# Forgetting attention from DRAM rows: split keys and queries, rounded value products, eight score groups a head

## The reference, cut to what matters

```python
k = rms_norm(k.reshape(N, T, N_HEADS, HEAD_DIM), k_norm)
q = rms_norm((xn @ w_q[j]).reshape(N, T, N_HEADS, HEAD_DIM), q_norm[j])
s = jnp.einsum('nqhd,nkhd->nhqk', q, k, preferred_element_type=jnp.float32) * (HEAD_DIM ** -0.5)
s = s + (c_q - c_k)            # c: running sums of the log forget values, by head
s = jnp.where(causal, s, NEG_INF)
p = jax.nn.softmax(s, axis=-1)
return jnp.einsum('nhqk,nkhd->nqhd', p.astype(v.dtype), v)
```

## Time and profile before

| | us |
|---|---|
| runs: lowest, median, highest | 2987.47, 2991.85, 2993.87 |
| profiled execution, its own time | 2989.96 |
| its span, first to last instruction | 2987.8 |
| PE busy | 2810.3 |
| DVE busy | 1178.7 |
| ACT busy | 779.7 |
| POOL busy | 154.1 |

### The profile page before, as it was taken

One profiled execution on the slowest core, in us unless ns is written; L12 is line 12 of the kernel. 1 busy time (PEld: TensorE's weight loads), 2 busy tenths in 40 slices (PEclk: granted clock), 3 DMA queues, 4 the chain that ended last, 5 costly groups with the idle time before them and its releaser, 6 DMA issues.

```text
span 2987.8 us, 41222 instructions
## 1 busy us (share of the span) xinstructions
PE 2810.3 (94%) x16738; PEld 2701.7 (90%) x16738; DVE 1178.7 (39%) x1258; ACT 779.7 (26%) x1163; POOL 154.1 (5%) x97
## 2 busy tenths in 40 slices
PE   6999999999999999999878888857999999999999
PEld 5999999999999999889876777745899999999998
DVE  4444434233142233433356666534344233242331
ACT  4111121111011122462454444434321011111111
POOL 3000020000000002110111000000010000000000
PEclk8999999999999999999998898979999999999999
DMA  3111111111111111123200111033011111111112
GB/s 96 48 46 42 43 51 42 43 43 49 42 42 49 43 43 47 39 72 86 54 28 20 53 26 27 23 107 110 22 43 49 43 43 49 42 42 44 47 42 73
DMA packets 251776, 145.79 MB, mean 49 GB/s; under 512 B 29424, under 2 KB 243248, under 8 KB 251682
## 3 DMA queue, kind: packets, MB, share of 16 engines
q1 hardware_dynamic: 232578, 135.47, 15.6%
q10 hardware_dynamic: 19104, 8.99, 1.1%
HBM read 130.91 MB, written 13.45 MB: 48 GB/s over the span
## 4 chain that ended last, share of the span: by engine, by line
PE 81%; DVE 6%; issue 4%; DMA 3%; ACT 3%; POOL 2%; ACTq 1%; SPq 0%; DVEq 0%; POOLq 0%
PE ps L377 71%; PE ps L655 3%; DMA inv_sums<-inv_rows 2%; DVE max_parts L593 2%; PE ps L820 1%; PE ps L743 1%; PE ps L631 1%; PE ps L632 1%; POOL t L412 1%; DMA inv_rows<-inv_spread 1%; DVE q_all L683 1%; DVE q_lo_hi L517 1%; DVE k_hi_lo L521 1%; DVE row_max L593 1%; POOL squares L1346 1%
## 5 line engine op out<-in xcount | busy, mean ns | idle before, releaser
L362 DVE TENSOR_TENSOR w_lo<-w_raw,w_hi 128x1024 fp32r<-128x1024 f32 x192 | 246.7, 1285 | 1259.5 <-ACT w_hi L354 1259.5
L377 PE MATMUL ps<-x_hi,w_hi 128*128 128x358 f32 x2688 | 593.9, 329 | 16.8 <-DVE x_lo L405 16.7
L377 PE MATMUL ps<-x_hi,w_lo 128*128 128x358 f32 x2688 | 590.9, 328 | 0.0
L377 PE MATMUL ps<-x_lo,w_hi 128*128 128x358 f32 x2688 | 589.4, 327 | 0.0
L354 ACT ACTIVATE w_hi<-w_raw 128x1024 fp32r<-128x1024 f32 x192 | 203.6, 1060 | 1322.8 <-PE ps L377 1320.4
L377 PEld LDWEIGHTS ps<-x_hi,w_hi 128*128 128x128 f32 x2688 | 465.2, 190 | 20.3 <-DVE x_lo L405 10.4
L377 PEld LDWEIGHTS ps<-x_lo,w_hi 128*128 128x128 f32 x2688 | 466.6, 190 | 0.0
L377 PEld LDWEIGHTS ps<-x_hi,w_lo 128*128 128x128 f32 x2688 | 466.4, 190 | 0.0
L377 PE MATMUL ps<-hid_hi,w_hi 128*128 128x358 f32 x1920 | 423.4, 329 | 3.2 <-DVE hid_lo L1150 3.2
L377 PE MATMUL ps<-hid_hi,w_lo 128*128 128x358 f32 x1920 | 420.8, 327 | 0.0
L377 PE MATMUL ps<-hid_lo,w_hi 128*128 128x358 f32 x1920 | 420.0, 327 | 0.0
(11 more groups left out here) (215 smaller groups left out, 2166.2 us busy)
## 6 DMA issues: line engine op xcount, KB each, us to landing
w_raw<-in_mlp_w SPq DMA_DIRECT2D x128, 512.0 KB, 4.0
w_raw<-in_conv_w_in SPq DMA_DIRECT2D x24, 512.0 KB, 3.8
w_raw<-in_w_kv SPq DMA_DIRECT2D x16, 512.0 KB, 3.8
k_page<-in_cache_k SPq DMA_DIRECT2D x16, 512.0 KB, 3.8
v_page<-in_cache_v SPq DMA_DIRECT2D x16, 512.0 KB, 4.0
inv_sums<-inv_rows SPq DMA_DIRECT2D x16, 260.0 KB, 3.4
w_raw<-in_conv_w_out SPq DMA_DIRECT2D x8, 512.0 KB, 3.9
out_k_prompt<-out_tiles ACTq DMA_DIRECT2D x8, 512.0 KB, 3.9
```

The source lines that it names most:

```text
L362: dve.tensor_tensor(WL[:, s], RAW[:, s], WH[:, s].bitcast(F32), ALU.subtract).then_inc(w_lo, 1)
L377: mm = pe.matmul(PS[:, G * s + g, 0:GW], w[:, s, k], x[:, k, g * GW:(g + 1) * GW], start=(k == 0 and n == 0), stop=(k == KC - 1 and n == 2))
```

## The change

- When a unit of keys or queries is normed, it is split at once: ACT rounds it into a staging tile (`stage_hi`), DVE takes the rest (`stage_lo`), and SP stores both to DRAM (`stage_out`, rows of `kh_rows`, `kl_rows`, `qh_rows`, `ql_rows`). Two pairs of staging tiles take turns. Only the decode tokens of the keys are kept in SBUF (`KSS`).
- The squares are made on ACT, twice: plain, and rounded. One activation table for logarithm and exponential is loaded ahead of the key stage.
- The four tiles of a head are fetched from DRAM by eight DMAs (`load_head`), in place of DVE's splits. The second half's tiles lie where the staging tiles lay, so that they are laid out on POOL (`extend(1)`) only when the last store has landed.
- Values come for two heads at a time into one float32 tile, and are split into `VH` (ACT) and `VL` (DVE). Probabilities are made by two exponentials, float32 and rounded, and DVE takes the difference. The value product is three matmuls of rounded parts.
- The 18 steps of a head become eight groups of two or three key blocks; a group's scores take two PSUM banks of two pairs, and one exponential covers them. The maximum pass has a ring of two banks in place of three.
- Values and sums are copied out together (`OS`). The inverse is taken at group 4 and the divide at group 7 of the next head.

```diff
+GROUPS = [
+    [piece(0, 0, 0, 0), piece(0, 1, 1, 0), piece(0, 2, 1, 256)],
+    [piece(1, 0, 0, 0), piece(1, 1, 1, 0)],
+    [piece(1, 2, 0, 0), piece(1, 3, 1, 0)],
+    [piece(1, 4, 0, 0), piece(1, 5, 0, 256)],
+    [piece(2, 0, 0, 0), piece(2, 1, 1, 0)],
+    [piece(2, 2, 0, 0), piece(2, 3, 1, 0)],
+    [piece(2, 4, 0, 0), piece(2, 5, 1, 0)],
+    [piece(2, 6, 0, 0), piece(2, 7, 0, 272), piece(2, 8, 1, 0)],
+]
+USE_AT = [(0, 1, 2), (3, 4), (5, 6, 7), (8, 9, 10), (11, 12), (13, 14, 15), (16,), (17,)]
+SHIFT_AT = {3: "A", 5: "B", 7: "C"}
+RING = 2
+HI_RING = 3
...
+        def logits(t):
...
+            ge(pe, h_done, ops_done(t - 2))
...
+        def exp_logits(t):
+            h, g = divmod(t, NG)
+            act.wait_ge(st_done, t + 1)
+            ge(act, l_done, ops_done(t - 2))
+            act.activation(wide(PF[:, t % 2], t), wide_logits(t), ACT.Exp, scale=SCALE).then_inc(e_done, 1)
...
+            ge(act, pv_done, t - 2)
+            act.activation(wide(PBH[:, t % HI_RING], t), wide_logits(t), ACT.Exp, scale=SCALE).then_inc(h_done, 1)
...
+        def probs_lo(t):
...
+            dve.tensor_tensor(PBL[:, t % HI_RING, 0:nb * w], PF[:, t % 2, 0:nb * w],
+                              PBH[:, t % HI_RING, 0:nb * w].bitcast(F32), ALU.subtract).then_inc(l_done, 1)
...
+        def weigh_values(t):
...
+                pe.matmul(to, VH[:, hh, j], ph, start=(j == 0), stop=False)
+                pe.matmul(to, VL[:, hh, j], ph, start=False, stop=False)
+                mm = pe.matmul(to, VH[:, hh, j], pl, start=False, stop=last)
...
+            def load_head(h):
+                _, hh = head(h)
+                own, other = halves(hh)
+                o, rows = other.start, slice(HD * h, HD * h + HD)
+                ge(sp, st_done, NG * (h - 1))
+                for to, src in ((QA[hh][own], qh_rows), (CK[hh][own], kh_rows), (QB[hh][own], ql_rows),
+                                (QB[hh][other], qh_rows), (DK[hh][own], kh_rows), (DK[hh][other], kl_rows)):
+                    sp.dma_start(to.bitcast(F32), src[rows]).then_inc(h_loaded[hh], 16)
+                sp.dma_start(CK[hh][o + 1:o + 3].bitcast(F32), c_rows[h]).then_inc(h_loaded[hh], 16)
+                sp.dma_start(QA[hh][o:o + 1].bitcast(F32), CK[hh][o + 3:o + 4].bitcast(F32)).then_inc(h_loaded[hh], 16)
...
             for h in range(HEADS):
-                if 0 < h < HEADS - 1:
-                    load_c(h + 1)
-                    load_v(h + 1)
                 if h:
                     spread_sums(h - 1)
                     load_inverse(h - 1)
+                if h % 2 == 0 and h + 2 < HEADS:
+                    load_v(h // 2 + 1)
+                if h + 2 < HEADS:
+                    load_head(h + 2)
                 load_logf(h)
...
+            for t in range(NG * HEADS):
+                h, g = divmod(t, NG)
+                if t + 1 < NG * HEADS:
+                    probs_lo(t + 1)
+                if h + 1 < HEADS:
+                    for u in USE_AT[g]:
+                        max_turn(h + 1, u)
+                    if g == 3:
+                        values_lo(h + 1)
+                if h and g == 4:
                     invert_sums(h - 1)
+                if h and g == 7:
                     divide(h - 1)
...
+            def head_squares(u0, n):
+                z = n if u0 == U_K else KC + n
+                act.wait_ge(unit_read, u0 + n + 1)
+                ge(act, z_fin, z - 1)
+                act.activation(SQ[u0][n % 2][0][:, :], KW[:, n % 2], ACT.Square).then_inc(z_sq, 1)
+                ge(act, z_fin, z)
+                act.activation(T2R[:, :], KW[:, n % 2], ACT.Square).then_inc(z_hi, 1)
+            def stage_hi(n, src):
+                act.wait_ge(z_fin, n + 1)
+                ge(act, st_kept[n % 2], 32 * (n // 2))
+                act.activation(STH[n % 2][:, :], src, ACT.Copy).then_inc(st_hi, 1)
...
+            act.preload_act_table_set("natural_log_exp_and_others")
...
+            def stage_lo(n, src):
+                dve.wait_ge(st_hi, n + 1)
+                ge(dve, st_kept[n % 2], 32 * (n // 2))
+                dve.tensor_tensor(STL[n % 2][:, :], src, STH[n % 2][:, :].bitcast(F32), ALU.subtract)\
+                   .then_inc(st_lo, 1)
...
+            sp.wait_ge(c_stored, 32)
+            sp.wait_ge(ext_ready, 4)
+            load_head(0)
+            stage_out(2 * KC - 1)
...
+            load_v(0)
+            sp.wait_ge(st_kept[0], 32 * KC)
+            sp.wait_ge(st_kept[1], 32 * KC)
             sp.wait_ge(ext_ready, 9)
+            load_head(1)
```

More of the change, by code:

```diff
@@ L138, in trunk @@
         HL, _ = place("hid_lo", [P, KC, T], F32R)
-        KS, _ = place("k_all", [P, KC, T], offset=hid0)
+        QA, CK, QB, DK, o = [], [], [], [], hid0
+        for half in range(2):
+            if half:
+                staged = o
+            for tiles, name in ((QA, "q_hi_ext"), (CK, "k_hi_ext"), (QB, "q_lo_hi"), (DK, "k_hi_lo")):
+                x, o = place(f"{name}{half}", [P, NPR], F32R, offset=o)
+                tiles.append(x)
+        KSS, o = place("k_sample_t", [P, KC, NS], offset=o)
+        assert o <= hid1
+        STH, STL = [], []
+        for par in range(2):
+            for tiles, name in ((STH, "staged_hi"), (STL, "staged_lo")):
+                x, staged = place(f"{name}{par}", [P, NPR], F32R, offset=staged)
+                tiles.append(x)
+        assert staged <= o - 4 * KC * NS
         QS, _ = place("q_all", [P, KC, T], offset=hid1)
@@ new lines, in logits @@
+            ge(pe, h_done, ops_done(t - 2))
+            for c, j, q0, n, keys, bank, col in GROUPS[g]:
+                diagonal = q0 == P * j
+                b, k = 2 * (t % 2) + bank, slice(P * j, P * j + keys)
+                mm = pe.matmul(PS[0:keys, b, col:col + n], CK[hh][:, k], QA[hh][:, q0:q0 + n], start=True, stop=False)
+                mm = pe.matmul(PS[0:keys, b, col:col + n], DK[hh][:, k], QB[hh][:, q0:q0 + n], start=False,
+                               stop=not diagonal)
+                if diagonal:
+                    mm = pe.matmul(PS[0:keys, b, col:col + keys], MASK[:, 0:keys], IDR[:, 0:keys], start=False,
+                                   stop=True)
@@ L1744, in k_turn, with keys_kept @@
+            def keys_kept(n):
+                dve.wait_ge(aux_read, AX_K + 3 + 6 * n + G)
+                dve.wait_ge(ks_kept, n + 1)
+                dve.wait_ge(st_lo, n + 1)
+            for n in range(KC):
+                if n == 0:
+                    cut_unit(U_K + 2)
                     rms_inverse(2)
                     dve.wait_ge(conv_stored, 32)
-                if not first:
-                    dve.wait_ge(aux_read, AX_K + 3 + 6 * (c - 2) + 12 * i + G)
-                    dve.wait_ge(k_kept, c + 2 * i - 1)
```

517 lines of the change are left out of this document (232 added, 285 removed).

## The result

The changed kernel takes **3049.71 us** (median of 4 runs, 3049.36 to 3054.29), the kernel before 2989.66 beside it (2982.28 to 2993.87). The ratio is 1.0207 with a 95% interval of 1.0184 to 1.0231: slower by 60 us, where the prediction's sum had 15, and outside the range of 2950 to 3040. The profiled execution took 3054.29 us, 4.6 above the median; its span is 3052.5.

What follows compares the result with a forecast made beforehand. PE, busy 94% of the span, was taken as the bound. 2989.96 - 6.1 (key stage) + 21.7 (heads +24.5, less 2.8 set-up) - 0.4 (end) = 3005.2; with 1.9 for the median 3007 us, range 2950 to 3040.

Steps and rivals of the forecast that it cites:

- Mechanism: In the heads: PE waits once a head for the queries' and keys' DMA, with the clock at half behind it.
- signs with numbers: Expected in the trace: waits of 2 to 5 us, heads 25 us apart, key units 14.7 us, first reduction about 1566.
- load of a head: Heads: eight DMAs, 1.6 MB at about 300 GB/s (263 to 395), take 7.85 us, 9.75 in every second head.
- Path to the load's issue at full clock: Heads: first maximum matmul through PE, ACT, DVE and the inverse's issue on SP takes 14.0 us.
- The clock: Heads: the clock falls after PE's pause as it did before, costing 2.2 us a head.
- Head 0: First head, with no inverse ahead of its load: 21.5 us.
- Key stage: Key projection: PE's wait for the logarithm on ACT goes, -6.1 us, bounds 0 and -10.4.
- Set-up: End of query projection to the loop's first steady step: 2.8 us ahead, bounds +3 to -7.
- Value product: PE in a head: three rounded passes replace a four-pass float32 product, 18.35 - 1.5 = 16.85 us dense.
- rival A: Heads: the load is hidden, heads of 19.1 us with the clock up, 2926 us; chance 0.12.
- Rival C: Heads: rate of 263 GB/s, longer pause, clock down twice as long, 27 us a head, 3033 us; chance 0.18.
- behind them: After the heads: one copy instead of two before the last inverse, -0.4 us; decode and MLP unchanged.

Runs made afterwards that it cites:

- small load: Changed kernel, but from head 2 on the six large DMAs of a head's load move 16 of 1040 columns each: 2962.8 us.
- later maxima: Changed kernel with the maximum pass of the next head begun two groups later: 2973.67 us, ratio 0.9959.
- one-row run: Changed kernel, but from head 2 on each of the six large DMAs reads one DRAM row 64 times, same bytes: 3049.7 us.
- wide run: Changed kernel with four 64-partition transfers of a head's load made two of 128 partitions, with one more store per staged unit: 3029.23 us, ratio 1.012.
- clock kept up: Changed kernel with 70 dummy matmuls of 128 columns on PE ahead of the wait for the load in heads 2 to 15: 3039.84 us, ratio 1.0165.
- pass left out: Changed kernel without the third value product (v_hi with probs_lo): 3036.45 us; the same omission in the version with four moves: 2919.05 us.
- table alone: Kernel before with only the logarithm and exponential table named once ahead of the key stage: 2962.83 us, ratio 0.9914.
- version with four moves: Changed kernel with maxima two groups later, inverse at group 3, values fetched behind queries and keys, values rounded and split in group 5: 2943.84 us, ratio 0.9861.
- projection parts alone: Kernel before with both squares of a key or query unit on ACT and the logarithm and exponential table named once: 2959.06 us, ratio 0.9889.

## Why the prediction was wrong

The direction, the place and the mechanism were as forecast, the size was not. By the prediction's own steps:

- **Mechanism: right.** PE waits for the DMA of a head's queries and keys once a head, longer in every second head, the clock at half behind it; DVE's maxima hold it for 12.9 us in all in place of 36.4, and the table loads of the key stage are gone. The signs with numbers missed: waits of 3.8 to 9.0 us where 2 to 5 were forecast, heads 28.8 us apart (25), key units 13.8 (14.7), the first reduction at 1560.8 (1566). The small load and the later maxima (-87, -76 us) show that the wait, and not the added work, makes it slow.
- **The failed step: the load of a head, with its 1.6 MB "at about 300 GB/s", 7.85 us, and 9.75 in every second head.** From the first of its own issues that is 8.3 on the mean, since 1.0 us of the 9.75 is the values' issue; it took 10.8: **+2.5 us a loop**. The runs show why: six transfers into 64 partitions ran at about 200 GB/s with the DMA engines fully busy, below my lower bound of 263. The one-row run clears the reading side, and in the wide run the rate doubles. The 395 of my upper bound was the fastest cell of the inverse's load, which has the very shape of each of the six, 64 x 1040. Over its whole length that load showed far less, in the kernel before already:

```profile
1691.60:1693.20 1.60, 1.60 (x13) 1.29 (x11) 0.00 (x0) 0.41 (x2) 0.00 (x0) 1.00 0.69 165
```

165 GB/s at a share of 0.69 is about 240 at a full share, an estimate, and 1.6 MB at 240 are 6.7 us in place of 5.3: more than half of the miss was to be read there. The fit that I quoted from the Trainium skill ("DMA: Bandwidth & Descriptors", Anatomy of one DMA), 5.7 us, is one that the page gives for transfers of GpSimd's queue, and these are SP's; the trace has 10.8 and decides.

- **Path to the load's issue at full clock.** My steps gave 14.0 us, and 15.0 with the values' issues in every second head, 14.5 on the mean. With the clock kept up it is 14.7 to 14.8, and 16.0 to 17.0 with the values: 15.4 on the mean, +0.9. From the values' first issue to the load's it is 1.2 to 2.3 us there in place of 1.0, 1.6 on the mean, which is 0.3 of the 0.9. A pass left out takes 1.17 us from the loop, so PE is most of this path, as I had it. Where the rest sits, between PE, the reductions and SP, was not tried.
- **The clock.** 2.2 us a head forecast, 2.7 by the difference of the two runs: +0.5. The longer pause did not make it much worse.
- These three make 28.9 us of 25.0; by PE's starts the loop is 28.8, and 13 times the difference is +49.5. Head 0 took 24.6 (21.5) and the last two 33.3 (32.3): +4. The heads were forecast at 378.8 and took 432.4.
- **Key stage: "What goes is the wait for the logarithm: -6.1 us": too small by more than a factor of two.** By the last scaled query the changed kernel is 16.7 us ahead of before; my steps gave 6.1 + 3.1 = 9.2. A unit was held by ACT's round of the unit: without two loads of 1.28 it takes 13.8 us, with the table alone just as in the changed kernel, and 8 x 1.85 = 15 goes. I had priced the unit at 14.7, from the wait row alone.
- **Set-up: an error that hid the former.** From the end of the last query to the loop's start I had 1580.4 - 1555.6 = 24.8 us, it took 29.4. The last store landed 5.9 us after its issue (4.1 forecast), since it stood behind the load of head 0, the same slow transfers again; and from the first reduction to the loop it took 16.7 (14), for a reason that no run shows. The start came 2.9 us earlier than forecast: two errors of 7.5 and 4.6 us, of which the second hid most of the first, by luck.
- **Value product, -1.5 us a head.** With the load hidden, a head takes 20.74 us, against 19.1 that I took and 23.0 on the mean of the first 13 of before. So rival A (2926) had the right picture of what lies behind the wait, with heads 1.6 us too short; the version with four moves stands at 2943.8. Of the pass's own price, 2.4, the runs show 1.5.
- **Rival C** had the nearest end (3033), with a longer pause and the rate of 263 GB/s, which was still too high. Its other half, the clock down for twice as long, did not come: 2.7 us a head, where the forecast had 2.2.

Against the profiled execution, 3005.2 forecast and 3054.3 measured: +53.6 in the heads, -2.9 at their start, -1.2 behind them (-1.6 where -0.4 was forecast), together 49.5, where the difference is 49.1. The projection parts alone gain 31 us (2959), so by difference what the change does to the heads and the set-up costs some 90 (3049.7), until their order is changed.

## What to carry to other kernels

When tiles that were computed on chip come from DRAM instead, the load belongs where its consumer needs it last, not first: moving the first use back by two groups was worth 76 us, the wider transfers 20 to 26 while the load was waited for, and nothing once it was hidden. Price a transfer by rows of its own shape, the number of partitions first, and over a whole transfer, not by its fastest 0.2 us; if the trace has none, let the lower bound be lower than the slowest row of another shape. And price what an engine loses or gains in a loop by the loop's period against the next engine's own work: the wait row said 6.1 us, the period 15.

## What the runs showed of the hardware

- Loads of 64 x 1040 from DRAM into 64 partitions, several in a row, ran at 192 to 233 GB/s with the DMA share at 1.0; loads of 128 x 1040 into 128 partitions at 391 to 400 with the same share. Reading one DRAM row 64 times changed nothing. A single such load of 64 rows reached 395 in 0.2 us, and 165 at a share of 0.69 over its 1.6 us.
- SP took 0.60 us to issue a 64 x 1040 transfer, so six of them hold its queue for 3.7 us.
- 32 table loads of 1.28 us, gone by one line, were worth 22 us of 2984 [0.9882, 0.9946]. The compiler had put one ahead of each change between logarithm and exponential, though one table serves both: with it loaded once, no other load stands in the key stage of that run.
- A pause of PE costs a second time: behind a pause of 9 us the granted clock was 0.52 in the next five us, over all heads this cost 2.7 us a head by the difference of two runs. Filling only part of the pause with work (4.8 us) shortened the path by 1.1 us, and the time by nothing that is clear of noise.
